# Feed-forward layer of a hybrid encoder block: weight pieces, half of the combinations and the residual loaded at other times around the turn between two phases, and sums of the input made in the order of first use

## The reference, cut to what matters

```
x  = x + gate1 * mixed                               # (512, 2048)
h2 = modulate(rmsnorm(x, norm_mlp_g), shift2, scale2)
y  = square(relu(h2 @ w_ff1)) @ w_ff2                # w_ff1 2048 x 8192, w_ff2 8192 x 2048
x  = x + gate2 * y
```

## Time and profile before

| | |
|---|---|
| median of 3 runs | 2319.35 us (2312.15 to 2320.38) |
| profiled execution, its own time | 2319.03 us |
| its span, first to last instruction | 2317.0 us |
| mean granted TensorE clock | 0.981 |
| TensorE matmul busy | 2202.4 us (95%), 12452 matmuls |
| VectorE busy | 1774.3 us (77%) |
| ScalarE busy | 1026.1 us (44%) |
| DMA | 480.16 MB, mean 207 GB/s |

### The profile page before, as it was taken

The page is one execution under the profiler, slowest core; times in us unless marked ns, Lnnn a source line. Parts: engine busy times, 40 slices in busy tenths (PEclk is TensorE's granted clock), DMA queues, the critical chain, the costliest instruction groups (busy, mean ns, idle before and its releaser), DMA issues.

```text
span 2317.0 us, 31640 instructions
## 1 busy us (share of the span) xinstructions
PE 2202.4 (95%) x12452; PEld 1931.2 (83%) x12452; DVE 1774.3 (77%) x1945; ACT 1026.1 (44%) x1371; POOL 322.3 (14%) x183
## 2 busy tenths in 40 slices
PE   6999999999999999999999999999779999999999
PEld 6788888888877878889999999999667777877787
DVE  5877877766555875798988898888767888788787
ACT  5435454532355222556655555556333333333331
POOL 1004434343421544300000000000000000000000
PEclk9999999999999999999999999999889999999999
DMA  9965445544665696255665655746767545645541
GB/s 336 339 214 205 164 159 173 186 159 164 227 216 211 236 330 233 79 185 196 233 236 182 248 207 210 266 162 221 218 227 288 203 161 208 246 140 205 200 145 73
DMA packets 261329, 480.16 MB, mean 207 GB/s; under 512 B 18874, under 2 KB 105404, under 8 KB 258368
## 3 DMA queue, kind: packets, MB, share of 16 engines
q1 hardware_dynamic: 237136, 397.94, 49.9%
q10 hardware_dynamic: 24048, 80.23, 9.0%
HBM read 389.48 MB, written 88.63 MB: 206 GB/s over the span
## 4 chain that ended last, share of the span: by engine, by line
PE 57%; DVE 21%; DMA 9%; issue 7%; ACT 3%; SPq 1%; POOL 1%; DVEq 0%; ACTq 0%; POOLq 0%
PE ps L959 10%; PE ps L961 10%; PE ps L960 10%; DMA st<-in_w_ff 8%; DVE wlo L2860 6%; PE ps L1500 5%; PE ps L1501 5%; PE ps L1502 5%; PE ps L1456 2%; PE ps L1458 2%; PE ps L1457 2%; ACT whi L2016 2%; DVE tlo L2842 2%; DVE yacc L2942 2%; DVE acc L2956 1%
## 5 line engine op out<-in xcount | busy, mean ns | idle before, releaser
L1456 PE MATMUL ps<-hc,whi 128*128 128x256 f32 x1680 | 478.8, 285 | 20.1 <-DVE cb L2928 15.2
L1457 PE MATMUL ps<-hc,whi 128*128 128x256 f32 x1680 | 477.2, 284 | 0.0
L1458 PE MATMUL ps<-hc,wlo 128*128 128x256 f32 x1680 | 477.2, 284 | 0.0
L1500 PE MATMUL ps<-whi,ab 128*128 128x512 f32 x840 | 333.2, 397 | 44.6 <-DVE yacc L2942 30.3
L493 POOL TENSOR_TENSOR wlo<-wraw,whi 128x1024 fp32r<-128x1024 f32 (+3 forms) x116 | 286.8, 2484 | 481.8 <-ACT whi L488 442.9
L1456 PEld LDWEIGHTS ps<-hc,whi 128*128 128x128 f32 x1680 | 324.4, 193 | 23.1 <-issue 17.2
L2016 ACT ACTIVATE whi<-st 128x1024 fp32r<-128x1024 f32 x180 | 190.4, 1058 | 316.2 <-PE ps L1502 142.3
L1501 PE MATMUL ps<-wlo,ab 128*128 128x512 f32 x840 | 329.6, 392 | 0.0
L1502 PE MATMUL ps<-whi,ab 128*128 128x512 f32 x840 | 329.2, 392 | 0.0
L1457 PEld LDWEIGHTS ps<-hc,whi 128*128 128x128 f32 x1680 | 324.4, 193 | 0.0
L1458 PEld LDWEIGHTS ps<-hc,wlo 128*128 128x128 f32 x1680 | 324.3, 193 | 0.0
(11 more groups left out here) (361 smaller groups left out, 4030.2 us busy)
## 6 DMA issues: line engine op xcount, KB each, us to landing
wraw<-in_w_ff SPq DMA_DIRECT2D x128, 512.0 KB, 6.3
st<-in_w_ff SPq DMA_DIRECT2D x120, 512.0 KB, 9.2
araw<-in_w_ada SPq DMA_DIRECT2D x112, 512.0 KB, 6.7
a_d<-ring ACTq DMA_DIRECT2D x109, 512.0 KB, 5.0
ab<-a_d SPq DMA_DIRECT2D x105, 512.0 KB, 5.8
wraw<-in_w_in SPq DMA_DIRECT2D x72, 512.0 KB, 5.9
arawx<-in_w_ada SPq DMA_DIRECT2D x48, 512.0 KB, 4.6
wraw<-in_w_out SPq DMA_DIRECT2D x32, 512.0 KB, 7.6
```

The lines of the kernel that those rows point to most:

```text
L1456: pe.matmul(dst, w[0][:, c], hi, start=new, stop=False, skip_group_check=True)
L1457: pe.matmul(dst, w[0][:, c], lo, start=False, stop=False, skip_group_check=True)
L1458: ins = pe.matmul(dst, w[1][:, c], hi, start=False, stop=t == 3, skip_group_check=True)
L1500: pe.matmul(dst, hi, w[0], start=new, stop=False, skip_group_check=True)
```

## The change

`back_of` gives each form its own delay. Form 3 comes one block later in groups 0 to 14; in the one-block groups 15 and 16 it comes two blocks later (before: none), form 2 one (as before). Group 16's pieces are loaded right after group 15's last combinations. Half of group 17's combinations (the second place of `ab[q]`) is loaded in group 15, after each product, the other half in group 16. In the even groups a product's piece load stands ahead of the wait for that product and of its combination load. The gate vector's store and load move behind group 19; the wait for the stored combinations moves behind group 17, ahead of `vq`; the residual's four loads move behind groups 19, 21, 23 and 25. The sums of the input are made in the order 1, 2, 3, and 5 later; copied in the order 2, 1, 3, and 5 later; their low parts are made in the order 2, 1, 3, 5, the first just ahead of group 0 and the others at its steps 1, 3 and 5. Pieces 2 and 3 of group 0 wait for three sums instead of four.

```diff
@@ -170,15 +170,22 @@
 FORM_FOR = {3: (2, 6), 2: (2, 4), 1: (1, 2), 4: (3, 2)}
 
 
+def back_of(t, g):
+
+    if blocks_of(g) == 1:
+        return {3: 2, 2: 1}.get(t, 0)
+    return int(t == 3 and g < GROUPS_A)
+
+
 def forms_at(p):
 
     forms = []
     for t, (q, lead) in FORM_FOR.items():
-        for back in (0, 1):
+        for back in (0, 1, 2):
             at = p + lead - back
             key = FF_ORDER[at] if 0 <= at < len(FF_ORDER) else ("", 0, 0, 0)
             alone = key[0] == "W" and blocks_of(key[1]) == 1
-            if key[0] == "W" and key[2] == q and back == (alone and t == 2) and (t, key[3]) != (4, 1):
+            if key[0] == "W" and key[2] == q and back == back_of(t, key[1]) and (t, key[3]) != (4, 1):
                 forms.append((t, key[1], key[3]))
             elif back == 0 and t == 4 and key[0] == "W" and key[2:] == (5, 0) and not alone:
                 forms.append((4, key[1], 1))
@@ -762,7 +769,7 @@
                 if g == 0 and r < 2:
                     sp.wait_ge(lo_ready, N_FF + 4 + 2 * r + i + 1)
                 elif g == 0:
-                    sp.wait_ge(s_sum, SUM_0 + 4)
+                    sp.wait_ge(s_sum, SUM_0 + 3)
                 else:
                     og, oi = last_use(g, place_of(g, i))
                     sp.wait_ge(f_low, LO_AT["W", og, (2, 3, 5, 4)[r], oi])
@@ -786,9 +793,11 @@
                                            11 * 1024 + 1024 * (s // 16)]
                              .rearrange("p (w n) -> p w n", w=2)).then_inc(ada_loaded[4], 16)
 
-        def comb_load(g, q):
+        def comb_load(g, q, parts=(0, 1)):
 
             for i, c in enumerate(chunks_of(g)):
+                if i not in parts:
+                    continue
                 sp.dma_start(ab[q][:, :, 2 * i:2 * i + 2, :].rearrange("p a k n -> p a (k n)").bitcast(F),
                              a_d[:, c, q, :, :]).then_inc(ab_in[q], 16)
 
@@ -823,26 +832,36 @@
                     comb_load(g + 1, q)
             else:
                 piece_load(g + 1, 3)
-        sp.wait_ge(ada_read, 24)
-        sp.dma_start(g2_d.rearrange("(t p) -> p t", p=P), M[:, M_G2:M_G2 + KT],
-                     allow_slow_non_contiguous=True).then_inc(g_stored, 16)
-        sp.wait_ge(g_stored, 32)
-        sp.dma_start(g2[:, :], g2_d.partition_broadcast(P)).then_inc(g2_in, 16)
+        for r in range(4):
+            piece_load(GROUPS_A + 1, r)
         for g in range(GROUPS_A, LAST):
             turn = (g - GROUPS_A) % 2 == 1
-            if g == GROUPS_A + 1:
+            for q in SEQ:
+                if 3 <= TURN[q] < 7 and g > GROUPS_A:
+                    piece_load(g + 1, (1, 0, 2, 3)[TURN[q] - 3])
+                if turn or g == GROUPS_A:
+                    sp.wait_ge(blk_done, FF_AT["W", g, q, blocks_of(g) - 1] + 1)
+                if g == GROUPS_A:
+                    if q == SEQ[0]:
+                        stored_wait(PRODUCTS * 3)
+                    comb_load(g + 2, q, (1,))
+                elif g == GROUPS_A + 1:
+                    comb_load(g + 1, q, (0,))
+                elif turn:
+                    comb_load(g + 1, q)
+            if g == GROUPS_A + 4:
+                sp.wait_ge(ada_read, 24)
+                sp.dma_start(g2_d.rearrange("(t p) -> p t", p=P), M[:, M_G2:M_G2 + KT],
+                             allow_slow_non_contiguous=True).then_inc(g_stored, 16)
+                sp.wait_ge(g_stored, 32)
+                sp.dma_start(g2[:, :], g2_d.partition_broadcast(P)).then_inc(g2_in, 16)
+            if g == GROUPS_A + 2:
                 stored_wait(PRODUCTS * (CHUNKS - 1) + 4)
-            for q in SEQ:
-                if turn:
-                    sp.wait_ge(blk_done, FF_AT["W", g, q, blocks_of(g) - 1] + 1)
-                    comb_load(g + 1, q)
-                if 3 <= TURN[q] < 7:
-                    piece_load(g + 1, (1, 0, 2, 3)[TURN[q] - 3])
-            if g == GROUPS_A + 2:
                 sp.dma_start(vq[:, :, :, :].rearrange("p a b n -> p (a b n)").bitcast(F),
                              a_d[:, CHUNKS - 1, 0:4, :, :].rearrange("p a b n -> p (a b n)")).then_inc(vq_in, 16)
-                for n in range(4):
-                    sp.dma_start(xr[n][:, :, :], x1_d[:, 4 * n:4 * n + 4, :]).then_inc(xr_in[n // 3], 16)
+            if g in (GROUPS_A + 4, GROUPS_A + 6, GROUPS_A + 8, GROUPS_A + 10):
+                n = (g - GROUPS_A - 4) // 2
+                sp.dma_start(xr[n][:, :, :], x1_d[:, 4 * n:4 * n + 4, :]).then_inc(xr_in[n // 3], 16)
         for n in range(G_OUT):
             for p in range(2):
                 sp.wait_ge(blk_done, FF_AT["W", LAST, n, 1] + 1)
@@ -1428,7 +1447,7 @@
             bank = 3 * (g % 2) + (2 if q == 6 else 1 if q in (1, 5) else 0)
             pe.wait_ge(f_low, LO_AT["W", g, q, i])
             if g == 0 and i == 0 and q in (1, 2, 3, 5):
-                pe.wait_ge(s_lo, SUM_0 + (None, 1, 2, 3, None, 4)[q])
+                pe.wait_ge(s_lo, SUM_0 + (None, 2, 1, 3, None, 4)[q])
             if i == 0:
                 if q == 0 and g >= 2:
                     pe.wait_ge(f_last, g - 1)
@@ -2033,8 +2052,8 @@
 
         def sum_hi(i):
 
-            q = (1, 2, 3, 5)[i]
-            act.wait_ge(s_sum, SUM_0 + (1, 2, 4, 3)[i])
+            q = (2, 1, 3, 5)[i]
+            act.wait_ge(s_sum, SUM_0 + (2, 1, 3, 4)[i])
             act.activation(comb(q, 0), comb_raw(q), ACT.Copy).then_inc(s_hi, 1)
 
         def slot_of(c, q):
@@ -2114,10 +2133,11 @@
             act.activation(tile, tile, ACT.Square).then_inc(f_sq, 1)
         for b in (6, 7):
             ff_hi(("F", 0, b))
-        for i in range(4):
+        for i in range(3):
             sum_hi(i)
         for p in range(GB - 3, GB):
             ff_hi(FF_ORDER[p + 3])
+        sum_hi(3)
         act.wait_ge(blk_done, FF_AT["F", 0, GB - 1] + 1)
         act.wait_ge(ada_summed, 10)
         for m in range(CT):
@@ -2811,15 +2831,13 @@
 
         def sum_low(i):
 
-            q = (1, 2, 3, 5)[i]
+            q = (2, 1, 3, 5)[i]
             dve.wait_ge(s_hi, SUM_0 + i + 1)
             dve.tensor_tensor(comb(q, 1), comb_raw(q), comb(q, 0).bitcast(F), ALU.subtract).then_inc(s_lo, 1)
         dve.wait_ge(h2_raw, SUM_0 + KT)
         dve.tensor_tensor(comb_raw(1), u(1, 0), u(1, 1), ALU.add).then_inc(s_sum, 1)
         dve.wait_ge(s_sum, SUM_0 + 1)
         dve.tensor_tensor(comb_raw(2), comb_raw(1), u(0, 0), ALU.subtract).then_inc(s_sum, 1)
-        dve.wait_ge(s_sum, SUM_0 + 2)
-        dve.tensor_tensor(comb_raw(5), u(0, 1), comb_raw(2), ALU.subtract).then_inc(s_sum, 1)
         dve.wait_ge(blk_done, FF_AT["F", 0, 3] + 1)
         dve.tensor_tensor(comb_raw(3), u(0, 0), u(1, 0), ALU.subtract).then_inc(s_sum, 1)
 
@@ -2961,13 +2979,13 @@
             dve.wait_ge(blk_done, FF_AT["V", n, 1] + 1)
             dve.tensor_tensor(y, ps[:, base:base + 4, :], y, ALU.add).then_inc(y_dve, 1)
 
+        for p in range(GB - 2, GB):
+            step_forms(p)
+            step_low(p)
+        dve.wait_ge(s_sum, SUM_0 + 2)
+        dve.tensor_tensor(comb_raw(5), u(0, 1), comb_raw(2), ALU.subtract).then_inc(s_sum, 1)
+        dve.wait_ge(s_sum, SUM_0 + 4)
         sum_low(0)
-        for p in range(GB - 4, GB):
-            step_forms(p)
-            if p >= GB - 2:
-                step_low(p)
-            if p < GB - 1:
-                sum_low(p - GB + 5)
         for g in range(GROUPS_A):
             c = g
             first = GB + 14 * g
@@ -2975,6 +2993,8 @@
                 step_forms(first + s)
                 step_low(first + s)
                 if g == 0:
+                    if s in (1, 3, 5):
+                        sum_low((s + 1) // 2)
                     if s in (3, 4, 5):
                         a_low(0, (0, 4, 6)[s - 3])
                     if s in (4, 6, 7, 8):
```

## The result

The changed kernel takes 2302.61 us (median of four runs, 2297.93 to 2306.21), the kernel before beside it 2318.86 us: a ratio of 0.9934, 95% interval 0.9908 to 0.9961. That is 16 us faster where 35 were forecast; the time lies in the range, and just where rival 3 had put it (2299 to 2306).

The account below looks back on a forecast made before the run. TensorE was taken as busy nearly everywhere, its gaps due to VectorE waiting for late weight pieces. Turn -22.4, later groups -15.5, forms -2.3, start +4.8 sum to -35.4: 2284 us from 2319, range 2264 to 2304.

Parts of the forecast that it names:

- rival 3: Later groups: piece 2 lands no earlier; 2299, up to 2306 if group 17's piece takes 12.4 us; chance 0.17.
- The later groups: Groups 18 to 28: piece 2 ahead of two combination transfers makes form 3 2.6 to 2.8 us earlier; -15.5 us.
- All are covered: 15.5 us: Later groups: the earlier form 3 removes TensorE's gaps after it, 2.6 us per pair of groups; between 0 and 15.8.
- The turn: Groups 15 to 17: earlier pieces and combinations shorten VectorE's waits; (16,4) ends at 1678.6 instead of 1700.99, -22.4 us.
- The gate store: Gate pair moved behind group 19's loads: SyncE's wait of 15.2 us there at worst delays loads used later; nothing.
- The start: Near 990 us: TensorE's gap goes but reopens, VectorE idles 4.4 us; +4.8 us, bounds -6.8 to +4.8.
- The forms: Groups 0 to 14: form 3 one step later only moves VectorE's wait to the next split; -2.3 us.

Follow-up runs that it names:

- e3: Changed kernel with the weight pieces in groups 18, 20, ... 28 again behind the wait and the combinations of their product, as in the kernel before; 2298.89 us.
- e4: Changed kernel, but in groups 18, 20, ... 28 all four pieces of the next group go ahead of five of the seven combinations; 2280.56 us.
- e10: Changed kernel, but in groups 18 to 28 only the two combination transfers of product 1 go behind piece 2; 2304.20 us.
- e5: Changed kernel, but only the combinations of products 0 and 6 of group 15 stand ahead of its piece 3, instead of five; 2298.45 us.
- e2: Changed kernel, but the fifth sum and the first split of a sum come directly behind the third sum, where VectorE idles; 2302.63 us.
- e7: Changed kernel with form 3 of groups 0 to 14 back at its old step; 2310.76 us.

## Why the prediction was wrong

**The later groups: the failed step.** "Nine transfers of 0.524 MB from 1839.35 on take 12.1 us at 390 GB/s; with 1.7 us of start that is 1853.2, so form 3 comes 2.6 to 2.8 us earlier". The new order has nine transfers from piece 1 to the first block's piece 2, and so had the old one: it only had product 3's pair where product 2's now stands. The same sum for the kernel before therefore gives 1853.2 too, where its trace has 1855.96. The whole forecast gain of 2.6 to 2.8 us was the error of the formula, which was not held against the row at hand. Rival 3, with a chance of 0.17, had just this: the queue delivers the same bytes ahead. From piece 1 to form 3 there pass 16.6 us before (1839.35 to 1855.96) and 17.3 after (1825.03 to 1842.34). The error lies in the start of the burst. The formula has 4.4 us for the first two of the nine (1.7, which stands in no row, and 1.34 each) and 9.4 us for the seven behind them. Before, the second, issued at 1840.49, landed 5.6 us later, 6.7 us after piece 1 went out, and the seven took 9.8 us more. In the changed kernel it is 7.7 and 9.5 us. Issues and their time to landing, the second transfer and piece 2, first before, then changed:

```profile
wraw<-in_w_ff SPq DMA_DIRECT2D x1, 512.0 KB, 5.6
...
st<-in_w_ff SPq DMA_DIRECT2D x1, 512.0 KB, 7.4
...
wraw<-in_w_ff SPq DMA_DIRECT2D x1, 512.0 KB, 6.6
...
st<-in_w_ff SPq DMA_DIRECT2D x1, 512.0 KB, 11.6
```

Why the first two take so long no run shows. The Trainium skill ("DMA: Bandwidth & Descriptors", Queues, rings and completion order) says that a DMA engine consumes the descriptors of its ring in order; e3, e4 and e10 agree: counted from the addition ahead of it, form 3 starts 0.7, 5.1 and 2.5 us earlier than in the changed kernel, with none, all four and two of the combination transfers between piece 1 and piece 2 put behind piece 2.

"All are covered: 15.5 us" failed as well, and by itself: e10 brought piece 2 about as much earlier as forecast (2.5 us) and won nothing, because piece 3 was next. The prediction never asked what was late next in that place.

**The turn: two terms mis-sized.** "Landing is thus 1624.1 at best, 1628.4 at worst (the queue as full); I take 1625, nearer the first, since only transfers issued before 1616 stand ahead." Five combination transfers are just what was issued before 1616; the copy came at 1629.29, 4.3 us late and past even the worst case, and e5 shows that three of them were the reason (1624.94). For piece 2 of group 17, 6.5 us were taken and 8.4 measured (1669.56 to 1677.96); rival 3's 12.4 did not occur. The two make 6.2 of the 6.9 us by which the turn fell short. The rest of the mechanism was right: group 16's stall gone, gap ahead of (16,4), VectorE as the chain between.

**The gate store** was costed at nothing and cost nothing: SyncE waits 8.3 us for it in group 19 (15.2 before), and no gap follows.

**The start: right.** In the seven profiles with the change's start, group 1 comes 104.6 to 106.6 us after the first sum, in the five with the old one 100.0 to 100.7: about 5 us, forecast 4.8, with the 4.33 us of idle time ahead of it. At group 11 it is still 5 to 6 us on average (526.3 against 520.3 with moved forms, 530.0 against 525.1 without), so the lateness is not made up on the way. That the idle time is all of its source is not shown: e2 filled it and had only half back at group 1.

**The forms: right in kind, their size open.** The wait moved to the next split. From product 4 of group 1 to that of group 11, where the start drops out, three kernels without the moved form take 423.4 to 425.4 us and ten with it 418.8 to 422.7: 3.5 us less on average, where 2.3 were forecast. By the medians e7 puts it at 8.2 us; what makes the difference stays open.

The profiles' sum, -2.1 + 3.0 - 15.5 + 1.9, is -12.7; the medians differ by 16. The difference is within what the unchanged first 970 us vary from one profile to the next.

## What to carry to other kernels

Here a transfer's landing was set by what was queued ahead of it: issuing it some us earlier was worth nothing while the same transfers stayed ahead, and putting two later-needed ones behind it took their 2.5 us off the wait. Before forecasting with a rate, reproduce the landing time in the trace at hand with it, the start of the burst included. And when a stall is to go, look up when the next input of the same chain lands: here two pieces in a row had to be moved, and moving one won nothing.

## What was not expected of the hardware

The bursts of transfers here started well below the rate that they reached later: in the changed kernel 199 to 328 GB/s in the six us from 1826, 356 to 420 from 1832 to 1852 (the rates above); before, 223 to 338 in the six us from 1840, 379 to 408 over the ten from 1846. It isn't the kind of transfer: pieces and combinations were issued by turns from 1825.03 on, and in e4 the four blocks of pieces 2 and 3, with nothing between them, landed about 4.0 us from first to last (issued at 1820.81 and 1826.42, landed 7.2 and 5.6 us later), which is about 390 GB/s, as for combinations. What slows the start is not shown.

And an idle TensorE lost its clock, so that gaps cost more than their length: in the changed kernel, idle from 1674.74 on, the granted clock was 1.00 until 1678, 0.73 over the next 2 us, then 0.50, the lower of the two levels, and the first matmuls of (16,4) took 0.63 us each until 1685.58, later ones 0.39. Stage and TensorE's timeline of the changed kernel:

```profile
1682.00:1684.00 2.00, 2.00 (x6) 1.52 (x6) 2.00 (x3) 1.06 (x1) 0.00 (x0) 0.50 0.44 165
```

```profile
1682.59 0.63 PE L1521 MATMUL ps<-whi,ab 128*128 128x512 f32 x1
...
1686.60 0.39 PE L1520 MATMUL ps<-wlo,ab 128*128 128x512 f32 x1
```
